# Three gate column groups of another branch, moved from the RWKV pair's finish into its chunk scan as pieces of 256 columns

## The chip, the cores and the metric

The kernel runs on one core of one Trainium2 chip. The metric is the device time of one execution in microseconds. In this document PE is TensorE (PEld its weight loads), DVE is VectorE, ACT is ScalarE, POOL is GpSimd and SP is SyncE, whose queue issues nearly all DMAs.

## The reference, cut to what matters

The whole program is two transformer blocks over 1024 tokens of width 1024. The first block has three mixing branches; one is RWKV-7 with 8 heads of 64 channels. Each branch's output is multiplied by a sigmoid gate, and the gates are one more projection of the same normalised input `h`:

```
h = _rmsnorm(x, norm_mix[l])
p = h @ w_in[l]
p_rwkv, p_mla, p_diff, p_gate = jnp.split(p, IN_SPLITS, axis=-1)
o_rwkv = _rwkv7_mix(p_rwkv, ...)
gates = jax.nn.sigmoid(p_gate + b_gate[l]).reshape(B, S, N_BRANCHES, D_MODEL)
merged = (gates[:, :, 0] * (o_rwkv @ w_branch_rwkv[l])
          + gates[:, :, 1] * (o_mla @ w_branch_mla[l])
          + gates[:, :, 2] * (o_diff @ w_branch_diff[l]))
...
def step(state, inp):                       # inside _rwkv7_mix, once per token
    r_t, w_t, k_t, v_t, kk_t, b_t = inp
    sa = jnp.einsum('bhij,bhj->bhi', state, -kk_t)
    state = (state * w_t[:, :, None, :] + sa[..., None] * b_t[:, :, None, :]
             + v_t[..., None] * k_t[:, :, None, :])
    return state, jnp.einsum('bhij,bhj->bhi', state, r_t)
_, y = lax.scan(step, state0, xs)
mean = jnp.mean(y, axis=-1, keepdims=True)
var = jnp.mean(jnp.square(y - mean), axis=-1, keepdims=True)
y = ((y - mean) * lax.rsqrt(var + RWKV_GN_EPS)).reshape(B, S, RWKV_DIM) * ln_w + ln_b
```

All arithmetic is float32. The columns of `p_gate` that this case is about do not depend on the RWKV branch at all; they can be computed wherever `h` is there, as long as they lie in memory before the branches are merged.

## The kernel before, in words

Channels lie on the 128 partitions and tokens run along the free axis. `h` is held in SBUF as 8 slices (`KD` = 8) of 128 rows by 1024 tokens. A product of 128 output columns with 512 tokens (one half, `HALF` = 512) takes 8 matmuls that add up in one PSUM bank; in float32 each of these matmuls appears as two records in the trace, each with a weight load of its own.

The program is a row of stages. A stage (the helper at line 43) gives each engine its own instruction list and a set of semaphores; it ends with a barrier of all engines (lines 47 to 51), so a stage lasts as long as its slowest engine, the SP queue with its waits for DMA included.

The RWKV branch loops four times (`PAIRS`) over pairs of heads; a pair fills the 128 partitions, head `e` on 64 of them. In each turn of the loop:

- `rwkv_prepare` (line 1500) projects r, k and v, loads `gate_w` (the weights of three blocks of 128 gate columns), and computes gate groups 0 to 2 of six. A gate group is one block of 128 columns for one half of the tokens.
- `rwkv_solve` (line 1716) inverts the small triangular systems of the chunks.
- `rwkv_scan` (line 2045) runs over 16 chunks (`NCH`) of 64 tokens. PE multiplies the state with `w_turned` (line 2087, into banks 0 and 1), DVE makes z of it (line 2060), PE adds two products to a new state product (lines 2092 and 2097, banks 2 and 3 in turn), DVE makes the next state (line 2070), and PE makes the chunk's output with three more kinds of product (lines 2101, 2104 and 2105, banks 4 to 7). All of these are 64 by 64 tiles of PE, 64 columns long. Then ACT copies the output out of banks 4 and 5 (line 2112), and DVE adds banks 6 and 7 (line 2077).
- `rwkv_finish` (line 2115) normalises y: PE sums over the channels (line 2144), DVE centres (line 2159), ACT squares (line 2171), PE sums again (line 2148), ACT takes logarithm and exponential (lines 2173 and 2175), and then DVE, ACT, DVE and DVE finish (lines 2162, 2179, 2164 and 2165). SP loads the next pair's r, k, v weights (line 2127). Gate groups 3 to 5 are computed here: three matmuls of group 3 between the two sums, the other 21 behind them (line 2138, banks 4 to 6). ACT copies each group to SBUF (lines 2177 and 2182), and SP stores it to memory (line 2130) and waits for the stores (line 2132).

Each engine goes through its list in order, and the order is written out by hand in these functions. Nothing else sets it.

Of the kernel before, what the change touches and what calls it, by code (L numbers as in the profile page):

```python
# [1421 lines left out]
def rwkv(nc, T, A, h, out):  # L1422
# [9 lines left out]
    with ExitStack() as keep:  # L1432
# [42 lines left out]
        with nc.Fori(0, PAIRS) as hp, ExitStack() as one:  # L1475
            tm = one.enter_context(sbuf(nc, "token_major", [P, 4, NT, P]))
            kr = one.enter_context(sbuf(nc, "kt_rt", [P, NT, 2, P]))
            bk = one.enter_context(sbuf(nc, "bt_kd", [P, 2, S]))
            bonus = one.enter_context(sbuf(nc, "bonus", [P, S]))
            gate = one.enter_context(sbuf(nc, "gate", [P, S]))  # L1480
            end_decay = one.enter_context(sbuf(nc, "end_decay", [P, NCH]))
            par = one.enter_context(sbuf(nc, "pair_params", [P, 12]))
            mu, w0, a0, k_k, k_a, r_k, ln_w, ln_b, one_m_ka = (par[:, 0:3], *(par[:, i:i + 1] for i in range(3, 11)))
            rwkv_prepare(nc, T, A, h, hp, lora, tm, kr, bk, bonus, gate, end_decay, par, slots, gate_w)
            y = one.enter_context(sbuf(nc, "y", [P, S]))
            with ExitStack() as solve:
# [4 lines left out]
                rwkv_scan(nc, T, kr, tm, pairs, wt, u, end_decay, y)  # L1491
            rwkv_finish(nc, T, A, h, hp, y, bonus, gate, ln_w, ln_b, out, slots, gate_w)


def pair_gate_place(T, hp, g):
# [546 lines left out]
                                            ).then_inc(corner_done, 1)  # L2042


def rwkv_scan(nc, T, kr, tm, pairs, wt, u, end_decay, y):

    kt_tm, v_tm, b_end, k_end = (tm[:, i, :, :] for i in range(4))

    with sbuf(nc, "state", [P, 2, RD]) as state, sbuf(nc, "z", [P, NT, 2, RD]) as z:
        with stage(nc, "state_made", "z_product", "z_made", "state_product", "y_made", "y_kept", "y_even") as (
                block, state_made, z_product, z_made, state_product, y_made, y_kept, y_even):
# [25 lines left out]

            @block.tensor  # L2080
            def _(pe):
                for c in range(NCH):
                    t, rows = c // 2, slice((c % 2) * CH, (c % 2 + 1) * CH)
                    pe.wait_ge(state_made, c + 1)
                    for e in range(2):
                        ch = slice(e * RD, (e + 1) * RD)
                        mm = nc.tensor.matmul(T.ps[e][rows, 0:RD], wt[ch, t, rows], state[ch, c % 2, :], start=True, stop=True)
                    mm.then_inc(z_product, 1)
                    if c < NCH - 1:
                        for e in range(2):  # L2090
                            ch = slice(e * RD, (e + 1) * RD)
                            nc.tensor.matmul(T.ps[2 + c % 2][ch, 0:RD], k_end[rows, t, ch], v_tm[rows, t, ch], start=True, stop=False)
                    pe.wait_ge(z_made, c + 1)
                    if c < NCH - 1:
                        for e in range(2):
                            ch = slice(e * RD, (e + 1) * RD)
                            mm = nc.tensor.matmul(T.ps[2 + c % 2][ch, 0:RD], b_end[rows, t, ch], z[rows, t, e, :], start=False, stop=True)
                        mm.then_inc(state_product, 1)
                    for e in range(2):
                        ch, uu = slice(e * RD, (e + 1) * RD), e * NT + t  # L2100
# [3 lines left out]
                        nc.tensor.matmul(dst, v_tm[rows, t, ch], pairs[rows, uu, 1, 1, :], start=True, stop=False)  # L2104
                        mm = nc.tensor.matmul(dst, z[rows, t, e, :], pairs[rows, uu, 0, 1, :], start=False, stop=True)
                    mm.then_inc(y_made, 1)

            @block.scalar
            def _(act):
                act.wait_ge(y_made, NCH)  # L2110
                for j in range(2):
                    nc.scalar.activation(y[:, j * HALF:(j + 1) * HALF], T.ps[4 + j][:, :], ACT.Copy).then_inc(y_kept, 1)


def rwkv_finish(nc, T, A, h, hp, y, bonus, gate, ln_w, ln_b, out, slots, gate_w):

    with sbuf(nc, "square", [P, S]) as sq, sbuf(nc, "gate_out", [P, 3, HALF]) as gate_out:
        with stage(nc, "mean_made", "centred", "squared", "var_made", "logged", "inverted", "chain", "affine", "finished", "slots_loaded",
                   "gate_made", "gate_copied", "gate_stored") as (
                block, mean_made, centred, squared, var_made, logged, inverted, chain, affine, finished, slots_loaded, gate_made,  # L2120
                gate_copied, gate_stored):
            halves = [slice(j * HALF, (j + 1) * HALF) for j in range(2)]

            @block.sync
            def _(sp):
                for b_ in range(3):
                    sp.dma_start(slots[:, b_, :, :], weight_cols(A["w_in"][0], KD, hp * P + (P + b_ * RH * RD))).then_inc(slots_loaded, 16)
                for g in range(3, 6):
                    sp.wait_ge(gate_copied, g - 2)
                    sp.dma_start(pair_gate_place(T, hp, g), gate_out[:, g - 3, :]).then_inc(gate_stored, 16)  # L2130
                sp.wait_ge(slots_loaded, 48)
                sp.wait_ge(gate_stored, 48)

            @block.tensor
            def _(pe):
                def gate_part(g, first, end):
                    for q in range(first, end):
                        part = nc.tensor.matmul(T.ps[1 + g][:, :], gate_w[:, g // 2, q, :], h[:, q, (g % 2) * HALF:(g % 2 + 1) * HALF],
                                                start=(q == 0), stop=(q == KD - 1))
                    if end == KD:  # L2140
                        part.then_inc(gate_made, 1)
# [12 lines left out]
            @block.vector  # L2154
            def _(dve):
# [12 lines left out]
            def _(act):  # L2168
# [7 lines left out]
                act.wait_ge(gate_made, 1)  # L2176
                nc.scalar.activation(gate_out[:, 0, :], T.ps[4][:, :], ACT.Copy).then_inc(gate_copied, 1)
                act.wait_ge(chain, 1)
                nc.scalar.activation(y[:, :], y[:, :], ACT.Identity, scale=ln_w, bias=ln_b).then_inc(affine, 1)
                for g in (4, 5):  # L2180
                    act.wait_ge(gate_made, g - 2)
                    nc.scalar.activation(gate_out[:, g - 3, :], T.ps[1 + g][:, :], ACT.Copy).then_inc(gate_copied, 1)

# [1193 lines left out]
```

## Time and profile before

| | us |
|---|---|
| median of 3 runs | 5857.65 (5855.17 to 5862.76) |
| the profiled execution | 5859.76 |
| its span, first to last instruction | 5858.0 |
| PE busy | 4996.6 (85% of the span) |
| DVE busy | 1690.3 (29%) |
| ACT busy | 1304.2 (22%) |
| POOL busy | 551.7 (9%) |

The span is cut into 40 slices of 146 us on the profile's page. The RWKV loop lies in the slices 3 to 8. A digit is the busy share in tenths, and PEclk the clock that was granted to TensorE, in tenths of its full rate:

```profile
PE   6688888887988678999989858787888886999898
PEclk9898889898999779999999979888989998999999
```

Durations of matmul records include the way through the array, so records overlap: their cadence (start to start) is what they cost in a row, and it is read from merged rows as (length of the group minus length of one) divided by (count minus one).

### The profile page before, as it was taken

Reading aid. Unit: us, or ns where it says so; the run is one execution under the profiler, and the core shown is the slowest. Engines: PE = TensorE matmul, PEld = TensorE weight load, DVE = VectorE, ACT = ScalarE, POOL = GpSimd, SP = SyncE. Lnnn points to the kernel's source line nnn. Section 1 sums busy time; section 2 is a strip of 40 time slices with the busy share of each in tenths; the row PEclk is TensorE's granted clock in tenths of the full one; section 3 lists DMA queues with packets and bytes.
Section 4 is the critical chain, followed back from the end, with each engine's and each line's share of the span. In section 5 each row is a group of like instructions: output and inputs, shape, how many; then the busy total and the mean of one; then the engine's idle time right before and its main releaser. Section 6 shows DMA issues by size and latency. Waiting matters only on the chain. (4 is left out here: it accounts for less than half of the span.)

```text
span 5858.0 us, 68475 instructions
## 1 busy us (share of the span) xinstructions
PE 4996.6 (85%) x27313; PEld 2669.7 (46%) x27313; DVE 1690.3 (29%) x3078; ACT 1304.2 (22%) x2058; POOL 551.7 (9%) x443
## 2 busy tenths in 40 slices
PE   6688888887988678999989858787888886999898
PEld 2254564532634433444434325566655642444344
DVE  5433243213611520211100035544515611111101
ACT  2222122102410420222200112322314412222100
POOL 0020121000010010000000022122300002000000
PEclk9898889898999779999999979888989998999999
DMA  3501101110021020111123111110010001111111
GB/s 75 83 14 34 30 7 34 39 38 11 1 77 43 33 74 28 47 37 38 36 82 117 53 39 44 42 43 25 19 40 1 1 29 30 39 39 36 34 39 52
DMA packets 301955, 232.06 MB, mean 40 GB/s; under 512 B 30771, under 2 KB 266982, under 8 KB 301670
## 3 DMA queue, kind: packets, MB, share of 16 engines
q1 hardware_dynamic: 301706, 228.40, 13.9%
q8 instruction: 198, 3.24, 0.2%
q14 instruction: 51, 0.42, 0.0%
HBM read 203.69 MB, written 24.67 MB: 39 GB/s over the span
## 5 line engine op out<-in xcount | busy, mean ns | idle before, releaser
L624 PE MATMUL psum<-ffn_in,up_slots 128*128 128x512 f32 x2816 | 1213.0, 594 | 54.6 <-DMA up_slots<-in_w_up_dram 35.9
L624 PEld LDWEIGHTS psum<-ffn_in,up_slots 128*128 128x128 f32 x2816 | 536.5, 191 | 731.1 <-issue 731.1
L661 DVE SCALAR_TENSOR_TENSOR conv<-u,conv_cols_a,conv 128x1024 f32<-128x1024 f32 x88 | 113.0, 1285 | 983.7 <-ACT conv L643 983.7
L438 PE MATMUL psum<-hidden,w_slots 128*128 128x512 f32 x704 | 305.0, 596 | 16.8 <-DMA w_slots<-in_w_down_dram 16.8
L2258 PE MATMUL psum<-hidden,w_slots 128*128 128x512 f32 x704 | 306.0, 596 | 10.3 <-DMA w_slots<-in_ffn_w_down_dram 10.3
L640 ACT ACTIVATE u<-psum 128x512 f32<-128x512 f32 x176 | 105.3, 598 | 892.9 <-PE psum L624 892.9
L2784 PE MATMUL psum<-h,w_slots 128*128 128x512 f32 (+1 forms) x576 | 217.4, 537 | 38.5 <-issue 36.3
L675 POOL TENSOR_TENSOR hidden<-conv 128x1024 f32 x44 | 103.2, 2346 | 1317.0 <-DVE conv L665 1317.0
L438 PEld LDWEIGHTS psum<-hidden,w_slots 128*128 128x128 f32 x704 | 134.6, 191 | 187.2 <-issue 169.6
L2258 PEld LDWEIGHTS psum<-hidden,w_slots 128*128 128x128 f32 x704 | 133.9, 191 | 177.1 <-issue 166.5
L1542 PE MATMUL psum<-x,w_slots 128*128 128x512 f32 x384 | 175.2, 620 | 34.2 <-issue 23.9
L2784 PEld LDWEIGHTS psum<-h,w_slots 128*128 128x128 f32 x576 | 112.1, 196 | 141.2 <-issue 136.2
L452 DVE SCALAR_TENSOR_TENSOR x<-psum,mods,x 128x512 f32 x32 | 24.0, 751 | 413.9 <-PE psum L438 413.9
L1542 PEld LDWEIGHTS psum<-x,w_slots 128*128 128x128 f32 x384 | 76.2, 200 | 133.2 <-issue 133.2
L1197 PE MATMUL psum<-x,w_slots 128*128 128x512 f32 x256 | 112.5, 603 | 14.4 <-DMA w_slots<-in_w_in_dram 14.4
L557 PE MATMUL psum<-branch,branch_slots 128*128 128x512 f32 x256 | 114.6, 611 | 11.5 <-DMA branch_slots<-in_w_branch_diff_dram 5.9
L744 PE MATMUL psum<-constants,gqa_logits 128*128 128x128 f32 x640 | 88.6, 276 | 41.9 <-DVE gqa_turned L802 21.8
L1091 DVE TENSOR_SCALAR reached<-pos_row,edge 128x128 f32<-128x128 f32 (+7 forms) x256 | 115.6, 515 | 28.3 <-PE psum L1115 28.1
L493 PE MATMUL psum<-x,gate_slots 128*128 128x512 f32 x256 | 112.8, 599 | 9.3 <-DMA gate_slots<-in_w_in_dram 9.3
L438 PE MATMUL psum<-merged,w_slots 128*128 128x512 f32 x256 | 113.0, 605 | 5.4 <-DMA w_slots<-in_w_o_dram 5.4
L324 PE MATMUL psum<-squares,constants 128*128 128x512 f32 x156 | 85.1, 710 | 27.2 <-ACT squares L313 27.2
L786 DVE CUSTOM_DVE_ANT_0 gqa_logits<-psum,no_bias 128x1280 f32<-128x1280 f32 x64 | 92.9, 1489 | 51.8 <-PE psum L2505 51.8
(553 smaller groups left out, 7475.1 us busy)
## 6 DMA issues: line engine op xcount, KB each, us to landing
mod_slots<-in_w_mod_dram SPq DMA_DIRECT2D x12, 2048.0 KB, 8.1
up_slots<-in_ffn_w_up_dram SPq DMA_DIRECT2D x44, 512.0 KB, 3.9
up_slots<-in_w_up_dram SPq DMA_DIRECT2D x44, 512.0 KB, 3.9
w_slots<-in_w_in_dram SPq DMA_DIRECT2D x38, 512.0 KB, 5.2
w_slots<-in_ffn_w_down_dram SPq DMA_DIRECT2D x8, 1408.0 KB, 12.4
w_slots<-in_w_down_dram SPq DMA_DIRECT2D x8, 1408.0 KB, 6.9
rows_in<-in_x_dram SPq DMA_DIRECT2D x16, 512.0 KB, 3.3
gate_w<-in_w_in_dram SPq DMA_DIRECT2D x16, 512.0 KB, 6.3
```

The costliest lines, as they stand in the source:

```text
L438: last = nc.tensor.matmul(T.ps[2 * s + j][:, :], slots[:, s, k, :], rhs(k)[:, j * HALF:(j + 1) * HALF], start=(k == 0), stop=(k == kt - 1))
L493: last = nc.tensor.matmul(T.ps[b][:, :], slots[:, s, k, :], rhs[:, k, j * HALF:(j + 1) * HALF], start=(k == 0), stop=(k == kt - 1))
L557: last = nc.tensor.matmul(T.ps[b][:, :], bslots[:, s, k, :], o[:, k, j * HALF:(j + 1) * HALF], start=(k == 0), stop=(k == KO - 1))
L624: last = nc.tensor.matmul(T.ps[b][:, :], slots[:, q, k, :], h[:, k, j * HALF:(j + 1) * HALF], start=(k == 0), stop=(k == KD - 1))
L640: nc.scalar.activation(u[:, q, lead + j * HALF:lead + (j + 1) * HALF], T.ps[b][:, :], ACT.Copy).then_inc(kept[b], 1)
L661: nc.vector.scalar_tensor_tensor(out=conv[:, q, :], in0=u[:, q, first:first + S], scalar=conv_w[first][:, bass.ds(col, 1)], in1=conv[:, q, :],
L675: nc.gpsimd.tensor_tensor(out[:, bass.ds(i * 2 + s, 1), :], conv[:, 2 * s, :], conv[:, 2 * s + 1, :], ALU.mult).then_inc(done[s], 1)
L1091: nc.vector.tensor_scalar(reached[:, n % RING, 0:w], pos_row[:, 0:w], edge[:, t, i:i + 1], None, ALU.is_le).then_inc(reached_made, 1)
L1197: last = nc.tensor.matmul(T.ps[b][:, :], slots[:, s, k, :], h[:, k, j * HALF:(j + 1) * HALF], start=(k == 0), stop=(k == KD - 1))
L1542: last = nc.tensor.matmul(T.ps[2 * b_ + j][:, :], slots[:, b_, q, :], h[:, q, j * HALF:(j + 1) * HALF], start=(q == 0), stop=(q == KD - 1))
L2258: last = nc.tensor.matmul(T.ps[bank][:, :], slots[:, b % 2, k, :], rhs[:, k, j * HALF:(j + 1) * HALF], start=(k == 0), stop=(k == KF - 1))
L2784: last = nc.tensor.matmul(T.ps[bank][:, 0:wd], slots[:, slot_of[x], c, :], h[:, c, at:at + wd], start=(c == 0), stop=(c == KD - 1))
```

## The change: what it does

Gate groups 3 to 5 leave `rwkv_finish` and go into `rwkv_scan`. Each matmul of 512 columns is cut into two of 256 (`CTX` = 256), which makes 48 pieces (3 groups, 2 parts, 8 slices). Each of the 16 chunks issues three of them: one behind the product of line 2087 (2107 in the new file), and two behind the chunk's output products. The pieces fill bank 3 alone, which the state products gave up: these now use bank 2 for all chunks. ACT copies the bank out once per group, ahead of the copies of y in its list, and SP stores each group and waits for the stores in the scan's stage. The three semaphores and the `gate_out` buffer move along.

```diff
+def rwkv_scan(nc, T, h, hp, kr, tm, pairs, wt, u, end_decay, y, gate_w):
...
+            gate_pieces = [(g, part, k) for g in range(3) for part in range(2) for k in range(KD)]
+            @block.sync
+            def _(sp):
+                for g in range(3):
+                    sp.wait_ge(gate_copied, g + 1)
+                    sp.dma_start(pair_gate_place(T, hp, 3 + g), gate_out[:, g, :]).then_inc(gate_stored, 16)
+                sp.wait_ge(gate_stored, 48)
...
-                                                       scalar=end_decay[:, c:c + 1], in1=T.ps[2 + c % 2][:, 0:RD],
+                                                       scalar=end_decay[:, c:c + 1], in1=T.ps[2][:, 0:RD],
...
+                def gate_piece(i):
+                    g, part, k = gate_pieces[i]
+                    if g >= 1 and part == 0 and k == 0:
+                        pe.wait_ge(gate_copied, g)
+                    at = ((3 + g) % 2) * HALF + part * CTX
+                    piece = nc.tensor.matmul(T.ps[3][:, part * CTX:(part + 1) * CTX], gate_w[:, (3 + g) // 2, k, :], h[:, k, at:at + CTX],
+                                             start=(k == 0), stop=(k == KD - 1))
+                    if part == 1 and k == KD - 1:
+                        piece.then_inc(gate_made, 1)
...
                     mm.then_inc(z_product, 1)
+                    gate_piece(3 * c)
...
                     mm.then_inc(y_made, 1)
+                    gate_piece(3 * c + 1)
+                    gate_piece(3 * c + 2)
...
             def _(act):
+                for g in range(3):
+                    act.wait_ge(gate_made, g + 1)
+                    nc.scalar.activation(gate_out[:, g, :], T.ps[3][:, :], ACT.Copy).then_inc(gate_copied, 1)
                 act.wait_ge(y_made, NCH)
...
-def rwkv_finish(nc, T, A, h, hp, y, bonus, gate, ln_w, ln_b, out, slots, gate_w):
...
-                gate_part(3, 0, 3)
                 for j in range(2):
                     pe.wait_ge(squared, j + 1)
...
-                gate_part(3, 3, KD)
-                gate_part(4, 0, KD)
-                gate_part(5, 0, KD)
```

PE's list for one chunk of the scan, from the scan's first instruction on, in the kernel before (a row gives the line, the operation, the names written and read, and the tile):

```order
L2087 MATMUL psum<-state,w_turned 64x64 [waits state_made_3483]
L2087 MATMUL psum<-state,w_turned 64x64
L2092 MATMUL psum<-token_major 64x64 x2
L2097 MATMUL psum<-z,token_major 64x64 [waits z_made_3485]
L2097 MATMUL psum<-z,token_major 64x64
L2101 MATMUL psum<-kt_rt,state 64x64
L2104 MATMUL psum<-chunk_pairs,token_major 64x64
L2105 MATMUL psum<-chunk_pairs,z 64x64
L2101 MATMUL psum<-kt_rt,state 64x64
L2104 MATMUL psum<-chunk_pairs,token_major 64x64
L2105 MATMUL psum<-chunk_pairs,z 64x64
```

The same chunk in the changed kernel (`gate_w` rows are the pieces; `x` is the name under which `h` shows):

```order
L2107 MATMUL psum<-state,w_turned 64x64 [waits state_made_3484]
L2107 MATMUL psum<-state,w_turned 64x64
L2097 MATMUL psum<-x,gate_w 128x256
L2113 MATMUL psum<-token_major 64x64 x2
L2118 MATMUL psum<-z,token_major 64x64 [waits z_made_3486]
L2118 MATMUL psum<-z,token_major 64x64
L2122 MATMUL psum<-kt_rt,state 64x64
L2125 MATMUL psum<-chunk_pairs,token_major 64x64
L2126 MATMUL psum<-chunk_pairs,z 64x64
L2122 MATMUL psum<-kt_rt,state 64x64
L2125 MATMUL psum<-chunk_pairs,token_major 64x64
L2126 MATMUL psum<-chunk_pairs,z 64x64
```

One piece now stands between the product for z and the wait for z; two more (`L2097 ... x2`) follow this list ahead of the next chunk's L2107. So PE goes from 64 by 64 tiles to the full array twice a chunk, and back twice.

ACT's list over the end of the scan and the finish, as one piece of the difference:

```order
-L2112 ACTIVATE y<-psum 128x512 [waits y_made_3487]
-L2112 ACTIVATE y<-psum 128x512
+L2135 ACTIVATE gate_out<-psum 128x512 [waits gate_made_3491] x3
+L2138 ACTIVATE y<-psum 128x512 [waits y_made_3488]
+L2138 ACTIVATE y<-psum 128x512
-L2177 ACTIVATE gate_out<-psum 128x512 [waits gate_made_3860]
-L2179 ACTIVATE y<-y,pair_params 128x1024 [waits chain_3856]
-L2182 ACTIVATE gate_out<-psum 128x512 [waits gate_made_3860] x2
+L2186 ACTIVATE y<-y,pair_params 128x1024 [waits chain_3948]
```

The copies of the three groups now stand ahead of the two copies of y, and the finish has none.

## Rows read from the trace of the kernel before

**Rows 1.** Span and mean granted clock of the core.
```profile
core 0: 5858.0 us, clock 0.917
```

**Rows 2.** By stretch: length, busy PE, PEld, DVE, ACT, POOL, clock, DMA share, GB/s.
```profile
425.80:429.20 3.40, 2.84 (x127) 2.70 (x119) 1.29 (x2) 1.72 (x3) 0.00 (x0) 1.00 0.02 5
...
430.30:458.10 27.80, 24.01 (x376) 20.80 (x376) 8.83 (x31) 0.05 (x1) 0.00 (x0) 0.54 0.01 2
...
461.40:479.10 17.70, 17.64 (x35) 7.72 (x36) 5.06 (x5) 7.72 (x8) 0.00 (x0) 0.85 0.39 104
479.10:493.10 14.00, 9.25 (x22) 3.80 (x20) 0.00 (x0) 1.20 (x2) 0.00 (x0) 0.91 0.10 37
638.40:666.20 27.80, 23.93 (x376) 20.72 (x376) 8.84 (x32) 0.12 (x1) 0.00 (x0) 0.54 0.01 2
```

**Rows 3.** Timeline of PE, first chunk: start, length, engine, line, tile, count, wait.
```profile
430.35 0.27 PE L2087 MATMUL psum<-state,w_turned 64*64 64x64 f32 x2 [1.71 <-DVE state L2056]
...
430.46 0.23 PE L2087 MATMUL psum<-state,w_turned 64*64 64x64 f32 x2
430.48 0.32 PE L2092 MATMUL psum<-token_major 64*64 64x64 f32 x3
431.07 0.33 PE L2097 MATMUL psum<-z,token_major 64*64 64x64 f32 x4 [0.28 <-DVE z L2060]
...
431.52 0.28 PE L2105 MATMUL psum<-chunk_pairs,z 64*64 64x64 f32 x3
```

**Rows 4.** Timeline of ACT from the scan's end on.
```profile
458.05 1.08 ACT L2112 ACTIVATE y<-psum 128x512 f32<-128x512 f32 x2 [28.78 <-PE psum L2105]
...
466.62 1.28 ACT L2173 ACT_TABLE_LOAD   x1
470.36 1.11 ACT L2173 ACTIVATE square<-psum,constants 128x1024 f32<-128x1024 f32 x1 [2.46 <-PE psum L2148]
...
488.38 0.60 ACT L2182 ACTIVATE gate_out<-psum 128x512 f32<-128x512 f32 x1 [6.27 <-PE psum L2138]
```

**Rows 5.** Timeline of PE in the finish.
```profile
461.46 3.75 PE L2144 MATMUL psum<-y,constants 128*128 128x512 f32 x4 [3.44 <-PEq L51]
...
468.44 1.88 PE L2148 MATMUL psum<-square,constants 128*128 128x512 f32 x4
470.16 18.19 PE L2138 MATMUL psum<-x,gate_w 128*128 128x512 f32 x42
```

**Rows 6.** Timeline of DVE: the finish's last operation, and the next turn's first.
```profile
477.85 1.23 DVE L2165 TENSOR_TENSOR branch<-y,gate 128x1024 f32 x1
493.18 0.06 DVE L1625 MEMSET raw<- 128x1 f32 x1 [14.10 <-PEq L51]
```

**Rows 7.** DMA issues from 455 to 500 us: count, size, time to landing.
```profile
w_slots<-in_w_in_dram SPq DMA_DIRECT2D x3, 512.0 KB, 5.5
...
gate_store<-gate_out SPq DMA_DIRECT2D x3, 256.0 KB, 2.0
```

**Rows 8.** 256 columns on the full array: weight loads in time, and the group by form.
```profile
3568.10 1.27 PEld L2784 LDWEIGHTS psum<-h,w_slots 128*128 128x128 f32 x6 [0.24 <-issue]
...
L2784 PE MATMUL psum<-h,w_slots 128*128 128x256 f32 x192 | 43.4, 379 | 0.0
```

**Rows 9.** Two places where the tile form changes; durations are min/median/max ns.
```profile
3070.79 0.59 PE L2246 MATMUL psum<-constants,term_rows 128*128 128x2 f32 x4
3071.30 1.06 PE L2267 MATMUL psum<-mod_slots,cond_pairs 128*32 128x512 f32 x8
...
L2246 PE MATMUL psum<-constants,term_rows x96: 251/251/272, 3070.3 to 3327.6; 128*128 128x2 f32 x96
...
3981.85 0.72 PE L2821 MATMUL psum<-gdn_q,gdn_k 128*128 128x128 f32 x5
3982.50 0.56 PE L2830 MATMUL psum<-constants,gdn_inv_t 64*64 64x64 f32 x12
...
L2821 PE MATMUL psum<-gdn_q,gdn_k x64: 275/275/422, 3616.6 to 4163.4; 128*128 128x128 f32 x64
```

More of the change, by code:

```diff
@@ L1490, in rwkv @@
                 rwkv_solve(nc, T, kr, bk, tm, pairs, wt, u)
-                rwkv_scan(nc, T, kr, tm, pairs, wt, u, end_decay, y)
-            rwkv_finish(nc, T, A, h, hp, y, bonus, gate, ln_w, ln_b, out, slots, gate_w)
+                rwkv_scan(nc, T, h, hp, kr, tm, pairs, wt, u, end_decay, y, gate_w)
+            rwkv_finish(nc, T, A, hp, y, bonus, gate, ln_w, ln_b, out, slots)
 def pair_gate_place(T, hp, g):
@@ L2042, in _ @@
                                             ).then_inc(corner_done, 1)
-def rwkv_scan(nc, T, kr, tm, pairs, wt, u, end_decay, y):
+def rwkv_scan(nc, T, h, hp, kr, tm, pairs, wt, u, end_decay, y, gate_w):
     kt_tm, v_tm, b_end, k_end = (tm[:, i, :, :] for i in range(4))
-    with sbuf(nc, "state", [P, 2, RD]) as state, sbuf(nc, "z", [P, NT, 2, RD]) as z:
-        with stage(nc, "state_made", "z_product", "z_made", "state_product", "y_made", "y_kept", "y_even") as (
-                block, state_made, z_product, z_made, state_product, y_made, y_kept, y_even):
+    with sbuf(nc, "state", [P, 2, RD]) as state, sbuf(nc, "z", [P, NT, 2, RD]) as z, sbuf(nc, "gate_out", [P, 3, HALF]) as gate_out:
+        with stage(nc, "state_made", "z_product", "z_made", "state_product", "y_made", "y_kept", "y_even", "gate_made", "gate_copied",
+                   "gate_stored") as (
+                block, state_made, z_product, z_made, state_product, y_made, y_kept, y_even, gate_made, gate_copied, gate_stored):
+            gate_pieces = [(g, part, k) for g in range(3) for part in range(2) for k in range(KD)]
[5 more added lines that the diff above has]
+                sp.wait_ge(gate_stored, 48)
             @block.vector
@@ L2091, in _ @@
                             ch = slice(e * RD, (e + 1) * RD)
-                            nc.tensor.matmul(T.ps[2 + c % 2][ch, 0:RD], k_end[rows, t, ch], v_tm[rows, t, ch], start=True, stop=False)
+                            nc.tensor.matmul(T.ps[2][ch, 0:RD], k_end[rows, t, ch], v_tm[rows, t, ch], start=True, stop=False)
                     pe.wait_ge(z_made, c + 1)
@@ L2096, in _ @@
                             ch = slice(e * RD, (e + 1) * RD)
-                            mm = nc.tensor.matmul(T.ps[2 + c % 2][ch, 0:RD], b_end[rows, t, ch], z[rows, t, e, :], start=False, stop=True)
+                            mm = nc.tensor.matmul(T.ps[2][ch, 0:RD], b_end[rows, t, ch], z[rows, t, e, :], start=False, stop=True)
                         mm.then_inc(state_product, 1)
@@ L2112, in _, with rwkv_finish @@
                     nc.scalar.activation(y[:, j * HALF:(j + 1) * HALF], T.ps[4 + j][:, :], ACT.Copy).then_inc(y_kept, 1)
-def rwkv_finish(nc, T, A, h, hp, y, bonus, gate, ln_w, ln_b, out, slots, gate_w):
[L2117 to L2121, printed above, removed]
+def rwkv_finish(nc, T, A, hp, y, bonus, gate, ln_w, ln_b, out, slots):
+    with sbuf(nc, "square", [P, S]) as sq:
+        with stage(nc, "mean_made", "centred", "squared", "var_made", "logged", "inverted", "chain", "affine", "finished", "slots_loaded") as (
+                block, mean_made, centred, squared, var_made, logged, inverted, chain, affine, finished, slots_loaded):
             halves = [slice(j * HALF, (j + 1) * HALF) for j in range(2)]
@@ L2127, in _ @@
                     sp.dma_start(slots[:, b_, :, :], weight_cols(A["w_in"][0], KD, hp * P + (P + b_ * RH * RD))).then_inc(slots_loaded, 16)
-                for g in range(3, 6):
-                    sp.wait_ge(gate_copied, g - 2)
-                    sp.dma_start(pair_gate_place(T, hp, g), gate_out[:, g - 3, :]).then_inc(gate_stored, 16)
                 sp.wait_ge(slots_loaded, 48)
-                sp.wait_ge(gate_stored, 48)
             @block.tensor
             def _(pe):
[L2136 to L2141, printed above, removed]
                 for j in range(2):
                     nc.tensor.matmul(T.ps[j][:, :], T.head_ones[:, :], y[:, halves[j]], start=True, stop=True).then_inc(mean_made, 1)
-                gate_part(3, 0, 3)
                 for j in range(2):
@@ L2175, in _ @@
                 nc.scalar.activation(sq[:, :], sq[:, :], ACT.Exp, scale=-0.5).then_inc(inverted, 1)
-                act.wait_ge(gate_made, 1)
-                nc.scalar.activation(gate_out[:, 0, :], T.ps[4][:, :], ACT.Copy).then_inc(gate_copied, 1)
                 act.wait_ge(chain, 1)
                 nc.scalar.activation(y[:, :], y[:, :], ACT.Identity, scale=ln_w, bias=ln_b).then_inc(affine, 1)
-                for g in (4, 5):
-                    act.wait_ge(gate_made, g - 2)
-                    nc.scalar.activation(gate_out[:, g - 3, :], T.ps[1 + g][:, :], ACT.Copy).then_inc(gate_copied, 1)
 N_MOD = 6
```

## The prediction, written before the changed kernel was run

> **What bounds the kernel now.** I read the span and the clock of the core first: 5858.0 us, mean clock 0.917 [rows 1]; the profiled execution took 5859.76, 1.8 more than its span and 2.1 above the median of 5857.65. So PE is granted nearly its full rate on the average, and the change touches places where it isn't. Next comes the table by stretch [rows 2]. The scan of the first pair lasts 27.8 us and the second pair's the same, with the same 376 matmul records; the loop turns four times, and I work out one pair and take it by four. In the scan PE's records are busy 24.01 of 27.80 us, but the clock is 0.54: nearly all of it runs at the lower level, 1.2 GHz. Third, the timelines. The scan is a chain: PE makes the product for z (L2087) at 430.35 and can go on with L2097 at 431.07, since DVE makes z between [rows 3]. From 430.35 to ACT's first copy of y at 458.05 [rows 3, 4] are 27.70 us for 16 chunks, 1.73 each. The finish has two ends. DVE's chain of normalisation ends at 477.85 + 1.23 = 479.08 [rows 6]. PE's gate group runs on to 470.16 + 18.19 = 488.35 [rows 5], ACT copies it until 488.98 [rows 4], the store lands after 2.0 [rows 7], and the next turn starts at 493.18 [rows 6]. So PE's 21 gate matmuls behind the sums end last there, 9.9 us behind DVE, and this tail is what the change can take away. The price is paid in the scan, whose length is set by PE's order and DVE's two small operations in turn.
>
> **What goes from the finish.** From PE's start at 461.46 [rows 5] to the next turn's start at 493.18 [rows 6] are 31.7 us. Without gates three things go. (1) The tail behind DVE's end: the last copy ended at 488.98 and the next turn came 4.2 later, 2.0 of them the store [rows 7] and 0.15 its issue. So the barrier and the way back to the loop's start cost about 2.1 us, and they stay. (2) The three gate matmuls between the two sums. The squares are ready at 466.62, when ACT turns to its table load, but the second sums start at 468.44 [rows 4, 5]. Without the gates PE starts the first of them once the means are through, at about 465.0. If the clock is at its lower level, each half takes 1.7 (two records at 0.85), the second ends at about 468.4, and the logarithm, at 470.36 before, starts near 468.6: 1.7 earlier. At the full clock the table load, which ends at 467.90 [rows 4], decides: 2.4 earlier. (3) The first copy of a gate group ahead of L2179 costs ACT nothing that DVE waits for; I take zero. The new length is then 479.08 - 461.46 - 1.7 + 2.1 = 18.0 us, a saving of 13.7; with a clock that is still up in the means it is 14.6. I take **14.0**. The loads of the next weights don't end the stage: they land 5.5 us behind their issue [rows 7], long before DVE is through. If that cover failed, the end would move by no more than those 5.5.
>
> **What a piece costs.** Weight loads for 256 columns follow each other at (1.27 - 0.19) / 5 = 0.216 us, where 0.19 is the length of one [rows 8]. A piece is two records, 0.43 at the full clock, and 0.86 at half.
>
> **What the scan's own records cost around it.** At the full clock, from the first chunk: L2087 takes 0.11 from first to last start, L2092 0.20 (430.37 to 430.58), and the block from L2097 to the last L2105 0.52 (431.07 to 431.58) [rows 3]. Before, z is ready 0.72 after L2087's first start.
>
> **The change of the tile form.** The full array and 64 by 64 tiles never follow each other in the scan before, so I bound the change by two other places. Five records of L2821 (full array) start at 3981.85, 0.11 apart ((0.72 - 0.28) / 4); the last starts at 3982.29, and the first 64 by 64 record follows at 3982.50 [rows 9]: 0.21 instead of 0.11, so 0.10 for the change. The other way round has only a relative: four records of L2246, 0.11 apart, the last starting at 3071.13, and the first of another tile form at 3071.30 [rows 9]. With 2 columns there is no streaming to speak of, so the change into another form takes 0.18 from the last short record. From below both can cost nothing, if the queue hides them under the records before; from above I double them. I take 0.18 into a piece and 0.10 out of it, the rows' own values.
> The Trainium skill speaks against the change here: by TensorEngine Tiling (Array Packing), Key Properties, going from one tiling mode to another drains TensorE. By that rule each of the four changes costs something; the trace agrees with 0.10 for one direction, and for the other no row here is exact. Without the rule a chunk would be 0.56 shorter.
>
> **One chunk, at the full clock.** L2087 0.11, change 0.18, piece 0.43, change 0.10, L2092 0.20, on to L2097 0.05, block 0.52, change 0.18, two pieces 0.86, change 0.10: 2.73 us. z is wanted at 1.07, past the 0.72 at which it is ready: DVE's work for z is now wholly covered, and so is its new state, made while two pieces run. PE alone sets the pace, and what was a chain of 1.73 us becomes a queue of 2.73. Of the 0.71 that the first piece takes with its changes about half hides behind DVE; of the other two nothing does.
> Fifteen chunks: 41.0. The last has no L2092 and L2097: 0.82 to the output block, 0.40 in it: 1.2. **The end:** ACT's list has the third gate copy ahead of y's two. Behind the last output product come change 0.18, three of four records 0.65, the last 0.38 long [rows 8], and the copy, 0.60 as in [rows 4]: y's copies start 1.86 after the products, where they used to start at once. **The bank:** pieces 16 and 32 wait for the copy of bank 3. Piece 15 stands in the z place of chunk 5, piece 16 behind that chunk's output, 1.0 later, which covers most. Pieces 31 and 32 are neighbours behind chunk 10, so there PE waits for 0.38 + 0.60 + some 0.08 less a cadence of 0.22: 0.85, with the next chunk's L2087 queued behind it. The stores go while the scan runs; the third lands 2.0 after its copy, as DVE's two additions end: nothing.
> Sum: 41.0 + 1.2 + 1.9 + 0.85 = 44.9 against 27.7, so **+17.2** a pair. Using one bank for the state product instead of two costs nothing, since PE takes the next one only after DVE's new state, which has read the bank.
>
> **The clock.** That sum is at the full rate. At 425.80 to 429.20 PE's records are busy 2.84 of 3.40 and the clock is full [rows 2]; it falls in the scan after that, where PE waits for DVE in every chunk. In the new chunk PE issues nearly without a gap, more densely than in that row, so I take the full rate for all of the scan.
>
> **Sum.** +17.2 - 14.0 = +3.2 a pair, four pairs +12.8. From 5859.76 comes 5872.6, and against the median, 2.1 lower, **5870.5 us**. In effect the gates' 20.6 us a pair at full rate (24 matmuls at 0.86) were half under DVE's chain in the finish, and the scan has little room for them once it is at full clock.
>
> **Rivals.**
> (a) Cheap changes of form, the faster side. If weight loads run ahead and nothing is paid at the four changes, a chunk is 2.17: 15 x 0.56 = 8.4 less a pair, -33.6 in all: 5837. Midway, 0.28 a chunk, is 5854. It decides below 2.52 a chunk, where scan and finish cancel (3.2 / 15 = 0.21 below mine). For it: in the scan PEld is busy 20.80 us beside PE's 24.01 [rows 2], so loads do run beside matmuls. Against: [rows 9]. Chance 0.25 for 2.17 to 2.5, typically 5847.
> (b) Dearer changes: doubled, 3.29 a chunk, +33.6: 5904. For it: the form with 64 columns and 64 rows has no row in that direction, and a full weight load is 0.19 long. Chance 0.15, typically 5888.
> (c) The clock stays low in the scan. Then a chunk is about twice as long in its pieces and products, some 5.0, and the scan about 80 us: +39 a pair, 6013. Against it: the argument above. Chance 0.03.
> (d) Scan's end and finish gain more than I allow, by the full clock in both sums and a drop of the clock less elsewhere in the turn: up to 2 a pair each way, 8 in all. It is a spread on each case rather than one of its own.
> (e) Forecast, 2.55 to 2.9 a chunk: 5860 to 5882. Chance 0.57.
>
> **How the numbers follow.** A measurement of this kernel can tell about 0.2%, 11.7 us, from no change: 5846 and 5869.4 are the borders. The forecast lies just outside; its own spread puts 0.35 of the 0.57 above 5869.4 and 0.21 inside. (a) gives 0.15 faster and 0.10 inside; (b) and (c) 0.18 slower; 0.01 is left for something faster still. That makes faster 0.16, same 0.31, slower 0.53. The range of 8 in 10 cuts the lower half of (a) and the upper part of (b): 5843 to 5894; it takes in both signs, and the forecast's own is 5860 to 5882.
>
> **What would show it.** In the trace after: a period of 2.7 us between z operations of DVE; no wait of PE for z or state, but one of about 0.85 at the 32nd piece; clock 1.0 in the scan; from L2107's first start to ACT's copy of y about 45 us; the finish from PE's first sum to the next turn 17 to 18 us. A period of 2.2 would be (a), over 3.2 (b), and a clock near 0.5 (c).

## The result: slower by 0.3%

| | us |
|---|---|
| before, median of 7 runs | 5862.76 (5855.17 to 5865.18) |
| after, median of 7 runs | 5880.96 (5874.44 to 5885.27) |
| ratio after to before | 1.0033, 95% interval 1.0021 to 1.0044 |
| predicted | 5870.5 (5843 to 5894) |

The forecast was +12.8 us; measured are +18.2. A second set of runs of the unedited changed kernel, taken with e5 below, gave 5868.70 in 8 runs (5856.82 to 5883.76) against 5856.79, ratio 1.0027 (1.0014 to 1.0040). The changed kernel scatters over 27 us in these 8 runs; the kernel before scatters over 12 us in 15 runs beside them. That scatter turns out to belong to the explanation.

The scans and two of the finishes of the changed kernel by stretch, with the columns of [rows 2]:

```profile
430.30:483.00 52.70, 51.32 (x472) 34.05 (x472) 8.93 (x32) 1.66 (x3) 0.00 (x0) 0.84 0.03 11
647.90:693.00 45.10, 43.76 (x472) 29.74 (x472) 8.92 (x32) 1.65 (x3) 0.00 (x0) 1.00 0.04 13
...
1071.90:1117.10 45.20, 43.76 (x472) 29.75 (x472) 8.93 (x32) 1.72 (x4) 0.00 (x0) 1.00 0.04 13
486.60:501.10 14.50, 5.67 (x8) 1.58 (x8) 5.04 (x5) 7.24 (x7) 0.00 (x0) 0.64 0.43 108
696.60:711.90 15.30, 6.55 (x8) 2.16 (x8) 5.04 (x5) 7.23 (x7) 0.00 (x0) 0.61 0.41 103
```

Each scan lasts from DVE's first instruction to ACT's first copy of y. Three are 45.1 to 45.2 us at the full clock, against 27.8 [rows 2]. The first is 52.7, at a clock of 0.84. The finish (PE's first sum to DVE's end) is 14.5 and 15.3 against 17.6. What follows it is in DVE's timeline, with the columns of [rows 6]:

```profile
499.89 1.23 DVE L2174 TENSOR_TENSOR branch<-y,gate 128x1024 f32 x1
502.79 0.06 DVE L1625 MEMSET raw<- 128x1 f32 x1 [1.67 <-PEq L51]
```

The next turn starts 1.67 us behind DVE's end, where it was 14.10 [rows 6]. So a pair gains 2.4 to 3.1 in the finish and 12.4 behind it. For pairs 2 to 4 that is 14.9 together, and they pay 17.3 in a scan at the full clock and 0.2 on the way between the stages: a net of +2.6 a pair. The first pair paid 24.8 in its scan. The four turns together are 19.7 us longer by the profiles (scans +76.8, finishes -10.4, what follows them -49.7, the ways between +0.6, and r, k, v stages +2.4); the rest of the program, which the change does not touch, adds 4.1.

One chunk at the full clock, from PE's timeline of the changed kernel (columns of [rows 3]):

```profile
671.58 1.13 PE L2097 MATMUL psum<-x,gate_w 128*128 128x256 f32 x4
672.64 0.33 PE L2107 MATMUL psum<-state,w_turned 64*64 64x64 f32 x4
672.90 0.70 PE L2097 MATMUL psum<-x,gate_w 128*128 128x256 f32 x2
673.53 0.27 PE L2113 MATMUL psum<-token_major 64*64 64x64 f32 x2
...
674.10 0.28 PE L2126 MATMUL psum<-chunk_pairs,z 64*64 64x64 f32 x2
674.30 0.48 PE L2097 MATMUL psum<-x,gate_w 128*128 128x256 f32 x1
```

From 671.58 to 674.30, 2.72 us, PE has no idle time: no row bears a wait. The two pieces with the way back take 1.06 (671.58 to 672.64), L2107 and the first piece with its way in and out take 0.89 (to L2113 at 673.53), and the small products with the way in take 0.77.

Where the clock is low, and where PE waits for bank 3, shows in DVE's operations for z in the first pair:

```profile
439.14 0.28 DVE L2070 SCALAR_TENSOR_TENSOR z<-psum,u 64x128 f32<-64x128 f32 x1 [2.83 <-PE psum L2107]
...
444.03 0.29 DVE L2070 SCALAR_TENSOR_TENSOR z<-psum,u 64x128 f32<-64x128 f32 x1 [2.83 <-PE psum L2107]
...
454.81 0.28 DVE L2070 SCALAR_TENSOR_TENSOR z<-psum,u 64x128 f32<-64x128 f32 x1 [1.44 <-PE psum L2107]
...
457.54 0.29 DVE L2070 SCALAR_TENSOR_TENSOR z<-psum,u 64x128 f32<-64x128 f32 x1 [1.45 <-PE psum L2107]
...
465.73 0.28 DVE L2070 SCALAR_TENSOR_TENSOR z<-psum,u 64x128 f32<-64x128 f32 x1 [1.44 <-PE psum L2107]
...
469.42 0.29 DVE L2070 SCALAR_TENSOR_TENSOR z<-psum,u 64x128 f32<-64x128 f32 x1 [2.40 <-PE psum L2107]
```

The period is 4.89 us at the low clock and 2.73 at the full one. At chunk 11 DVE waits 2.40 instead of 1.44: 0.96 more, the wait of piece 32 for ACT's copy (0.85 forecast). At the scan's end ACT copies the third group at 482.53 and turns to y behind it:

```profile
482.53 0.60 ACT L2135 ACTIVATE gate_out<-psum 128x512 f32<-128x512 f32 x1 [14.17 <-PE psum L2097]
483.03 1.08 ACT L2138 ACTIVATE y<-psum 128x512 f32<-128x512 f32 x2
```

### The profile page after: what moved, and what is told of

Its sections match the earlier page's. It is cut to its first block and busy times, and to the rows that moved or that the text cites. A ratio compares the mean times of both kernels' runs of the same rounds, so it can differ in the third digit from the quotient of the medians.

```text
span 5881.8 us, 68859 instructions
## 1 busy us (share of the span) xinstructions
PE 5005.4 (85%) x27505; PEld 2676.5 (46%) x27505; DVE 1688.7 (29%) x3078; ACT 1304.5 (22%) x2058; POOL 551.9 (9%) x443
## 5 line engine op out<-in xcount | busy, mean ns | idle before, releaser
L493 PE MATMUL psum<-x,gate_slots 128*128 128x512 f32 x256 | 113.3, 601 | 14.9 <-DMA gate_slots<-in_w_in_dram 14.9
L2097 PE MATMUL psum<-x,gate_w 128*128 128x256 f32 x384 | 123.5, 430 | 2.7 <-ACT gate_out L2135 2.7
L744 PE MATMUL psum<-constants,gqa_logits 128*128 128x128 f32 x640 | 89.6, 279 | 41.4 <-DVE gqa_turned L802 21.7
```

The lines of the kernel that those rows point to most:

```text
L493: last = nc.tensor.matmul(T.ps[b][:, :], slots[:, s, k, :], rhs[:, k, j * HALF:(j + 1) * HALF], start=(k == 0), stop=(k == kt - 1))
L2097: piece = nc.tensor.matmul(T.ps[3][:, part * CTX:(part + 1) * CTX], gate_w[:, (3 + g) // 2, k, :], h[:, k, at:at + CTX], start=(k == 0), s ...
```

## The experiments

**e1_left_out: neither scan nor finish has the gates.** This takes the gains of the finish alone. Groups 3 to 5 are left out; their places in memory get copies of groups 0 to 2, which makes six stores instead of three in the stage of transposes inside `rwkv_prepare`.

```diff
-                    gate_piece(3 * c)
-                    gate_piece(3 * c + 1)
-                    gate_piece(3 * c + 2)
...
-                for g in range(3):
-                    act.wait_ge(gate_made, g + 1)
-                    nc.scalar.activation(gate_out[:, g, :], T.ps[3][:, :], ACT.Copy).then_inc(gate_copied, 1)
```

> Gate groups 3 to 5 are neither in the scan nor in the finish (left out; their places in memory get copies of groups 0 to 2, stored in the stage of transposes, where they should hide). Theory: the finish and its tail give back 14.7 us a pair, as in the trace after (2.4 in the chain, 12.4 in the tail), and the scan is again 27.8 us at the low clock: 59 us faster than before, some 5804. It follows that the scan's pieces cost 77 us in all. Rival: a part of the 14.7 comes from the full clock that the pieces leave behind in PE, and is lost without them: less than 50 us faster.

Measured: 5827.22 against 5857.48, ratio 0.9945 (0.9930 to 0.9959), 30 us faster and not 59. The first scan and finish, a later stage, and how that stage stood before:

```profile
429.30:457.10 27.80, 23.98 (x376) 20.77 (x376) 8.89 (x32) 0.02 (x1) 0.00 (x0) 0.54 0.01 2
460.60:475.80 15.20, 6.33 (x8) 1.98 (x8) 5.04 (x5) 7.23 (x7) 0.00 (x0) 0.61 0.41 103
...
3679.90:3825.60 145.70, 120.39 (x1652) 89.69 (x1652) 72.38 (x136) 44.64 (x66) 45.61 (x36) 0.91 0.10 32
```

And the kernel before, the same columns:

```profile
3730.20:3869.90 139.70, 119.36 (x1652) 89.93 (x1652) 74.28 (x135) 44.43 (x66) 45.67 (x36) 0.94 0.10 34
```

The first three rows are e1's, the last is the kernel before's, for the same stage of the second block: the same 1652 records, but 6.0 us longer at a clock of 0.91 instead of 0.94. In the touched stages theory holds: scan 27.8, finish 15.2 to 15.5, and 1.6 to 1.7 to the next turn, in all four pairs. That is 14.8 a pair, with none of it owed to a warmer PE, so that the rival falls. But 59 is gained in these stages and about 28 is lost elsewhere. Some 7 of the 28 are this edit's own: the six stores end the stage of transposes later, so that PE's first product behind it waits longer. Here it is for the second pair in e1, and in the kernel before:

```profile
568.12 0.97 PE L1744 MATMUL psum<-kt_rt,bt_kd 64*64 64x128 f32 x6 [4.77 <-PEq L51]
...
583.10 0.67 PE L1744 MATMUL psum<-kt_rt,bt_kd 64*64 64x128 f32 x6 [1.51 <-PEq L51]
```

Over the four pairs these waits are 2.56, 4.77, 2.96 and 2.69, against 1.64 and three times 1.51. The other 21 or so lie in stages that no edit touched, where, as in the row above, the clock was low for longer. I had not allowed for such a size: a change's worth in its stages and in the whole differ here by some 20 us.

**e5_after_again: the changed kernel, unedited, in another execution.** There is no edit, so no diff.

> The changed kernel once more, unedited, for a second profile. In the first one the scan of pair 1 took 52.7 us at clock 0.84 and those of pairs 2 to 4 45.15 at 1.00. Theory: the clock's fall in pair 1 belongs to where the chip's own clock decisions fall in the program, so another execution may have it in another pair or in none; each scan is 45.15 where the clock is 1.00, and the whole varies by the 7.5 us of such a scan. Rival: it is tied to the program (the first turn has a longer way to its scan), and pair 1 is slow again by the same amount.

```profile
426.50:471.60 45.10, 43.76 (x472) 29.74 (x472) 8.92 (x32) 1.66 (x3) 0.00 (x0) 1.00 0.04 13
635.30:680.50 45.20, 43.76 (x472) 29.74 (x472) 8.93 (x32) 1.70 (x4) 0.00 (x0) 1.00 0.04 13
843.20:888.40 45.20, 43.76 (x472) 29.74 (x472) 8.94 (x32) 1.73 (x4) 0.00 (x0) 1.00 0.04 13
1051.30:1096.40 45.10, 43.76 (x472) 29.74 (x472) 8.89 (x32) 1.68 (x3) 0.00 (x0) 1.00 0.04 13
```

This time all four scans hold the full clock, the span is 5855.0, and the time, 5856.82, is the least of its eight runs. So the low clock of the first pair is not tied to the program: theory holds (the record does not say whether the first profile came from the same chip). One such fall is worth 7.5 us (52.7 less 45.2). It accounts for a part of the 27 us of scatter; the r, k, v stages of pairs 2 to 4 were 2 to 4 us shorter than in the first profile, too. Against the profile before, the touched stages cost 10.6 here, yet the span is 3.0 shorter (5855.0 against 5858.0): the stages not touched gave some 13 back.

**e2_cols64: pieces of 64 columns** (three quarters of the gate products are left out).

```diff
-                    piece = nc.tensor.matmul(T.ps[3][:, part * CTX:(part + 1) * CTX], gate_w[:, (3 + g) // 2, k, :], h[:, k, at:at + CTX],
+                    piece = nc.tensor.matmul(T.ps[3][:, part * CTX:part * CTX + 64], gate_w[:, (3 + g) // 2, k, :], h[:, k, at:at + 64],
```

> The changed kernel with pieces of 64 columns instead of 256 (three quarters of the gate products are left out; everything else, order, waits and copies, stays). It parts the price of the columns from that of the change of tile form. Theory: a piece's pass costs 0.053 instead of 0.216 at the full clock, so a chunk falls from 2.73 by 0.98 to 1.75 us; the chain with no pieces would be 1.43 at the full clock, and the 0.3 above it are the changes of form. Rival: the columns are all that costs, and then the period between two z operations is 1.43 to 1.5 us. If the clock falls, the period is over 2.5.

```profile
429.90:483.90 54.00, 52.53 (x472) 44.98 (x472) 8.93 (x32) 1.73 (x4) 0.00 (x0) 0.52 0.03 11
649.90:704.80 54.90, 53.56 (x472) 45.86 (x472) 8.93 (x32) 1.65 (x3) 0.00 (x0) 0.51 0.03 11
```

The scans fell to the low clock (0.51 and 0.52), and with a quarter of the columns they took 54 to 55 us, 9 to 10 more than with whole pieces at the full clock; the time of the one run was 5917.94. For the question of columns against trips this told nothing. For the clock it told much: less work for PE in a chunk, and the stretch is longer.

**e9_cols64_front: the same, held at the full clock** by three extra matmuls ahead of chunk 0 and whole pieces in chunks 0 to 2.

```diff
+                for k in range(3):
+                    nc.tensor.matmul(T.ps[3][:, 0:CTX], gate_w[:, 1, k, :], h[:, k, 0:CTX], start=True, stop=True)
                 for c in range(NCH):
...
+                    wide = CTX if i < 9 else 64
```

> As e2_cols64 (pieces of 64 columns; three quarters of the gate products left out), whose scans all fell to the low clock. Here three extra matmuls of 256 columns stand ahead of chunk 0, and the pieces of chunks 0 to 2 keep 256 columns, so that the clock stays up. Theory: where the clock is 1.00 the chunks from 3 on take 1.75 us, 0.98 less than 2.73 and 0.32 more than the 1.43 of a chunk without pieces: the two trips to the full array cost time that no column explains. Rival: trips are free, and the period is 1.43 to 1.5. If the clock falls again, 3.4 and nothing is told.

```profile
430.00:450.00 20.00, 20.00 (x259) 15.59 (x258) 4.83 (x17) 0.60 (x1) 0.00 (x0) 1.00 0.04 15
```

And DVE's timeline, its operations for z:

```profile
445.49 0.28 DVE L2070 SCALAR_TENSOR_TENSOR z<-psum,u 64x128 f32<-64x128 f32 x1 [0.96 <-PE psum L2110]
...
447.49 0.29 DVE L2070 SCALAR_TENSOR_TENSOR z<-psum,u 64x128 f32<-64x128 f32 x1 [0.97 <-PE psum L2110]
```

Up to 450 us the clock is 1.00 and the period 2.00 us. The rival, 1.43 to 1.5, is out: with a quarter of the columns a chunk is still far above that. But theory said 1.75. Four records of L2246, with only 2 columns each, start 0.11 apart [rows 9], and so do e9's records of 64 columns behind the first, while I had taken 0.053 for them. Going from 0.216 to 0.108 in each of six records takes 0.65 away and not 0.98, which gives 2.08. The last 0.08 is in the first record of each place: from it to the second are 0.32 us with 256 columns (0.70 less a length of 0.38, in the row of 672.90 above) and 0.16 with 64. So the 0.57 above 1.43 is the price of the trips and of six records at that pace; which has what share of it, this run doesn't tell.

Later in the scan the clock fell after all, in the stretch in which PE waits for ACT's copy of bank 3 (PE busy 2.31 of 3.00); the scan took 43.6 at 0.80:

```profile
454.00:457.00 3.00, 2.31 (x28) 1.82 (x24) 0.58 (x2) 0.60 (x1) 0.00 (x0) 0.81 0.17 60
```

**e6_three_behind_z: all three pieces in one place,** one trip a chunk.

```diff
-                    gate_piece(3 * c)
+                    for i in range(3 * c, 3 * c + 3):
+                        gate_piece(i)
...
-                    gate_piece(3 * c + 1)
-                    gate_piece(3 * c + 2)
```

> The changed kernel with all three pieces of a chunk behind the product for z, none behind the output: the same columns, one trip to the full array and back in a chunk instead of two. Theory: a trip costs some 0.30 us at the full clock, but the next product for z now waits for DVE's state again, so the chunk is 2.63 instead of 2.73 us (0.11 + 0.15 + 1.49 + 0.88), and y's copies start 1.3 us sooner behind the last chunk; against that two waits of 0.85 for the bank instead of one. The scan is 43.5 to 44 us at the full clock against 45.15. Rival: trips cost nothing and DVE's part is exposed: 2.73 or more, over 45.

```profile
427.50:470.70 43.20, 41.67 (x472) 30.99 (x472) 8.91 (x32) 1.68 (x3) 0.00 (x0) 1.00 0.04 14
```

And DVE's timeline, in a later pair's scan:

```profile
662.99 0.29 DVE L2070 SCALAR_TENSOR_TENSOR z<-psum,u 64x128 f32<-64x128 f32 x1 [0.43 <-PE psum L2107]
664.86 0.28 DVE L2080 SCALAR_TENSOR_TENSOR state<-state,end_decay,psum 128x64 f32<-128x64 f32 x1 [1.58 <-PE psum L2119]
665.58 0.28 DVE L2070 SCALAR_TENSOR_TENSOR z<-psum,u 64x128 f32<-64x128 f32 x1 [0.43 <-PE psum L2107]
```

The period is 2.59 (2.63 expected), the scans are 43.2 (43.5 to 44 expected), and the ratio to before is 1.0014 (1.0003 to 1.0025), with 5863.34 us. The same columns with half the trips are shorter by 0.14 a chunk, although DVE's state is now waited for. PE's row for the six records shows more: from 662.87 to L2114 at 664.37 they take 1.50, where the two places of the changed kernel took 0.63 and 1.06.

```profile
662.87 1.56 PE L2097 MATMUL psum<-x,gate_w 128*128 128x256 f32 x6
```

So one trip less saves 0.19 there for the same columns, and its way in comes on top. This shows the change of tile form as a cost of its own.

**e3_two_groups: two groups in the scan, one in the finish,** where DVE's chain covers it.

```diff
+            gate_pieces = [(g, part, k) for g in range(2) for part in range(2) for k in range(KD)]
+            at_z = [3, 3] + [2] * 13 + [0]
...
+                    for i in range(sum(at_z[:c]), sum(at_z[:c + 1])):
+                        gate_piece(i)
...
+                gate_part(5, 0, 1)
                 for j in range(2):
                     pe.wait_ge(squared, j + 1)
...
+                gate_part(5, 1, KD)
```

> Groups 3 and 4 in the scan, all pieces behind the product for z (3 in chunks 0 and 1, 2 in 2 to 14, none in 15); group 5 in the finish, one matmul between the two sums and seven behind. Theory: the chunk is 2.20 us (two pieces under DVE's z, one trip to the full array and back), the scan about 35 us, +7.3 a pair; the finish to the next turn 17.8 instead of 31.7 us: -13.9. Net -6.6 a pair, 26 us faster than before: 5836. Rival: what counts is the number of pieces times 0.43, wherever they stand; then the scan is 27.8 + 32 x 0.43 = 41.5 and the kernel no faster than before.

```profile
430.70:465.40 34.70, 34.10 (x440) 25.15 (x440) 8.94 (x32) 1.19 (x2) 0.00 (x0) 1.00 0.04 14
469.00:485.10 16.10, 13.31 (x24) 5.54 (x24) 5.06 (x5) 7.82 (x8) 0.00 (x0) 0.82 0.43 115
```

All four scans are 34.7 at clock 1.00, the finish is 16.1, and the next turn starts 2.2 behind it. That is +6.9 and -13.4 a pair. The time is 5832.32 against 5857.48, ratio 0.9956 (0.9944 to 0.9969): 25 us faster than before, as expected (26). The rival, 41.5 for the scan, falls. Thirty-two pieces cost 6.9 and the changed kernel's 48 cost 17.3, but the place explains little of that: e6 has its third piece in the same place as the two here, and its chunk is 2.59 instead of 2.15, the full 0.43 more. The second place adds only the 0.14 between e6 and the changed kernel.

**e8_two_even: the same with two pieces in every chunk** (`at_z = [2] * 16`).

> As e3_two_groups (groups 3 and 4 in the scan behind the product for z), but with two pieces in every chunk instead of three in chunks 0 and 1. Theory: the chunk stays 2.15 us and the scan 34.7 to 35.5 where the clock is 1.00; chunk 0 is thinner, so in some execution a scan may fall, as in e4: then 10 us more. The median lies between that of e3 (5832) and 8 us above. Rival: two pieces a chunk hold the clock wherever they stand, and the time is that of e3 within 2 us.

Measured: 5836.88 against 5862.83, ratio 0.9958 (0.9945 to 0.9972), all four scans 34.4 at clock 1.00. Two pieces a chunk hold the clock, in this profile and by the narrow runs (5835.27 to 5840.60), with no help at the start. The median is 4.6 above e3's, but the kernel before was 5.4 slower in this set of runs, too; against it e8 equals e3 (26.0 us faster and 25.2), as the rival has it.

**e4_one_group: one piece a chunk, two groups in the finish** (`at_z = [1] * 16`).

> Group 3 in the scan, one piece a chunk behind the product for z; groups 4 and 5 in the finish, one matmul between the sums and fifteen behind. Theory at the full clock: the chunk is 1.77 us, the scan 28.5, +0.7 a pair; the finish to the next turn 25 us, -6.7; net -6.0, 24 us faster: 5839. Rival: with one piece a chunk PE is too idle to hold the full clock, the chunk is 2.7 to 2.9 us, the scan 45, and the kernel 40 us slower than before. Mixed between pairs is possible: the clock of each scan tells.

```profile
427.40:468.80 41.40, 41.20 (x408) 29.02 (x408) 8.89 (x32) 0.63 (x2) 0.00 (x0) 0.53 0.00 1
641.50:669.00 27.50, 27.30 (x408) 18.99 (x408) 8.93 (x32) 0.51 (x1) 0.00 (x0) 1.00 0.01 2
843.40:870.90 27.50, 27.29 (x408) 18.99 (x408) 8.90 (x32) 0.54 (x2) 0.00 (x0) 1.00 0.01 2
1044.90:1086.00 41.10, 40.90 (x408) 28.91 (x408) 8.89 (x32) 0.64 (x2) 0.00 (x0) 0.53 0.00 1
```

Both cases stand side by side in one execution: identical code takes 27.5 us at the full clock, with a whole group in it and still less than the 27.8 without, and 41.4 at the low one. The runs go from 5860.14, the profiled one, to 5889.41, with the median at 5877.78; the ratio is 1.0036 (1.0024 to 1.0048). So one piece a chunk is free against the kernel before, if the clock is held. What pays for it is the clock, as e7 shows next.

**e7_front: that one with four pieces in chunk 0** (`at_z = [4] + [1] * 12 + [0] * 3`).

> As e4_one_group (group 3 in the scan behind the product for z, groups 4 and 5 in the finish), with four of the sixteen pieces in chunk 0, one each in chunks 1 to 12 and none in 13 to 15. In e4 the scans of pairs 2 and 3 kept the full clock and took 27.5 us, those of pairs 1 and 4 fell to the low clock and took 41.2 and 41.4. Theory: the fall comes from PE's idle time at the stage's start together with a thin first chunk; four pieces at once fill it, all four scans stay at 1.00 and take 27.5 to 28.5 us, and the kernel is 24 us faster than before. Rival: what decides is the activity in the chunks themselves, and one piece a chunk is too little: one or more scans over 40 us again, and the kernel no faster than before.

```profile
430.90:459.40 28.50, 27.40 (x408) 19.62 (x408) 8.88 (x32) 0.60 (x1) 0.00 (x0) 0.97 0.03 11
633.80:663.70 29.90, 28.71 (x408) 20.50 (x408) 8.93 (x32) 0.60 (x2) 0.00 (x0) 0.92 0.03 10
837.20:865.80 28.60, 27.39 (x408) 19.73 (x408) 8.93 (x32) 0.62 (x2) 0.00 (x0) 0.96 0.03 11
1038.80:1067.50 28.70, 27.49 (x408) 19.82 (x408) 8.94 (x32) 0.64 (x2) 0.00 (x0) 0.96 0.03 11
456.00:459.40 3.40, 2.70 (x43) 1.95 (x41) 0.95 (x4) 0.00 (x0) 0.00 (x0) 0.71 0.09 36
```

No scan stays at the low clock now. They take 28.5 to 29.9 (27.5 to 28.5 expected), and in the first, third and fourth the clock gives way only in the last chunks, which have no piece (last row, for the first). But in the second it did fall at the start, and came back while the four pieces ran; there the first chunk took 4.46 us instead of the others' 3.02:

```profile
634.90:638.30 3.40, 3.40 (x23) 2.38 (x23) 0.16 (x1) 0.00 (x0) 0.00 (x0) 0.50 0.00 0
638.30:656.00 17.70, 17.70 (x275) 12.45 (x272) 5.80 (x21) 0.00 (x0) 0.00 (x0) 1.00 0.01 2
```

The time is 5840.55 against 5862.83, ratio 0.9964 (0.9950 to 0.9978). Moving three pieces to the front turned 20 us slower (5877.78 against 5857.48) into 22 faster. Theory holds in part: a dense first chunk kept the clock up or brought it back, where in e4 a fall lasted for the scan. That the start alone decides is not shown. By e9 a dense start does not hold the clock through a later wait of PE, and only one execution of e7 was profiled, though its five runs lie within 9 us.

DVE's operations for z in the last chunks show what a piece costs at the full clock:

```profile
657.79 0.28 DVE L2071 SCALAR_TENSOR_TENSOR z<-psum,u 64x128 f32<-64x128 f32 x1 [0.43 <-PE psum L2108]
...
659.51 0.29 DVE L2071 SCALAR_TENSOR_TENSOR z<-psum,u 64x128 f32<-64x128 f32 x1 [0.43 <-PE psum L2108]
...
660.96 0.28 DVE L2071 SCALAR_TENSOR_TENSOR z<-psum,u 64x128 f32<-64x128 f32 x1 [0.43 <-PE psum L2108]
```

Chunk 12, with a piece, takes 1.72, and chunk 13, without one, 1.45. So a first piece costs some 0.28 a chunk and is not hidden; it comes out even with the kernel before because that one's chunks ran at the low clock, at 1.73 each.

## Why the prediction was right, step by step

- **What goes from the finish.** Forecast 14.0 a pair, measured 14.9 in pairs 2 to 4: 2.4 to 3.1 in the chain (1.7 to 2.4 forecast) and 12.4 behind it. The barrier and the way back cost 1.67, not 2.1. The upper case of 14.6 in the prediction is a slip: with 2.4 in the place of 1.7 its own terms give 14.4. Nothing hangs on it.
- **The chunk.** Forecast 2.73, measured 2.73. Its terms were less exact than the sum. The small products with the way in took 0.77, for 0.95 forecast: they run closer together than I had them (0.63 from L2113 to the last L2126, for 0.77). The pieces with their other changes and L2107 took 0.89 and 1.06, for 0.82 and 0.96: the second record of a piece starts 0.32 behind the first, 0.10 more than the cadence. The two errors cancel, and that is luck. The cost of changing the form, bounded from two foreign places, held in the sum; e6 and e9 show it as a cost of its own.

The Trainium skill says (TensorEngine Tiling (Array Packing), Key Properties) that a change of tiling mode drains TensorE. The runs agree in so far as a trip costs time, 2.59 with one and 2.73 with two; a drain as such no trace here shows.
- **The end and the bank.** The bank's wait was 0.96 (0.85 forecast). The scan from PE's first record to ACT's copy of y was 44.9 forecast; from DVE's first instruction, 0.17 earlier, it measured 45.15. That is right within 0.1.
- **The clock.** This is the term that was mis-sized. "I take the full rate for all of the scan" held in seven of the eight scans profiled, and the eighth cost 7.5 more. That the chip could be in either state with the same code, as e4 shows, was not in my cases: rival (c) had all scans low, or none. The rest of the 18.2 lies in stages not touched, or in more such falls; e1 shows that untouched stages can shift by some 21, more than the change's whole effect. That +18.2 came within 6 us of +12.8 is therefore in part luck.
- **The rivals.** (a) Free changes of form: out, by the 2.73 and by e9. (b) Dearer ones: out. (c) A low clock all through: out for this kernel, but true in e2. (d) The spread of the finish: 0.9 a pair, within its 2.

With the full clock everywhere the net is +2.6 a pair, some +10 in all, beside 12.8 forecast. What stays open: in which stage of an execution the clock falls, and so how much of the measured 18.2 is due to the scans. One execution with four clean scans took 5856.82, within the runs of the kernel before.

## What to carry to other kernels

The waits of a dependent chain do not by themselves make added work free. With none, one, two and three pieces of 256 columns behind the product for z, a chunk took 1.45, 1.72, 2.15 and 2.59 us at the full clock (e7's chunk 13, e4, e3, e6): some 0.28 for the first and 0.43 for each piece more. What made one piece a chunk cost nothing against the kernel before was that PE then could run at the full clock. Two cost 6.9 us a pair for 13.4 gained, three cost more than they gave back. Split the work between the two covers, instead of emptying one into the other: the best version left one group under the finish's own chain and was 25 us faster than before. And count the clock as a resource: a sparse stretch had better begin densely (e7), since in e4 the same code cost half as much again in two of four pairs. What the scan would take without pieces, were the clock full all through, no run here shows.

## What the runs showed of the hardware

- The same code ran at two levels of the clock within one execution: 27.5 us at 1.00 and 41.4 at 0.53 (e4). With a denser first chunk no scan stayed low; one fell at its start and was back at 1.00 before the first chunk ended (e7).
- Less PE work made a stretch longer: pieces with a quarter of the columns took 54 to 55 us at 0.51 to 0.52, whole ones 45.1 at 1.00.
- On the full array, records of 64 columns came no closer than those of 2 columns, 0.11 us apart (e9, [rows 9]). Going there from 64 by 64 tiles and back took some 0.3 us over the columns at the full clock, in three parts of about 0.1: the first piece record started 0.15 behind the last small one (0.06 between small ones), the second 0.32 behind the first (0.22 further on), and the next small one 0.31 behind the last piece record (672.33 to 672.64).
- Stages with identical instructions differed between kernels by up to 6 us in 140 (clock 0.91 and 0.94), so that a change of 59 us in its own stages showed as 30 in the whole; 7 of the missing 28 were a longer wait for stores that the edit itself had added (e1).
